# Two transformer layers and a mixture block in float32: the norms in front of the feed-forward parts are applied after the product instead of before it

## The reference, cut to what matters

```
def rms_norm(x, g):
    y = x * rsqrt(mean(x * x, axis=-1) + EPS)
    return y * g
def modulate(h, shift, scale):
    return h * (1 + scale) + shift
def swiglu(h, w_in, w_out):
    a, u = split(h @ w_in, 2)
    return (silu(a) * u) @ w_out

x  = x + g1 * (merged @ w_o)
h2 = modulate(rms_norm(x, norm2), sh2, sc2)
x  = x + g2 * swiglu(h2, w_ffn_in, w_ffn_out)
```

## Time and profile before

| | |
|---|---|
| median of 3 runs | 3013.39 us (3013.12 to 3019.73) |
| profiled execution, its own time | 3018.23 us |
| its span (first to last instruction) | 3016.3 us |
| TensorE busy | 2892.8 us, 96% of the span |
| mean granted TensorE clock | 0.985 of full |

### The profile page before, as it was taken

The page is one execution under the profiler, slowest core; times in us unless marked ns, Lnnn a source line. Parts: engine busy times, 40 slices in busy tenths (PEclk is TensorE's granted clock), DMA queues, the critical chain, the costliest instruction groups (busy, mean ns, idle before and its releaser), DMA issues.

```text
span 3016.3 us, 40764 instructions
## 1 busy us (share of the span) xinstructions
PE 2892.8 (96%) x16464; PEld 2148.1 (71%) x16464; DVE 954.1 (32%) x1413; ACT 959.0 (32%) x1668; POOL 800.2 (27%) x624
## 2 busy tenths in 40 slices
PE   8999889999999999999988999999999999999998
PEld 6887668888888888878766777888854644444444
DVE  3505551122211111051453123212367532322324
ACT  3226442123221122242544223222355331212114
POOL 2323222324222322443222444444420300000000
PEclk8999999999999999999999999999999999999999
DMA  5114321111111211212322222232220369999990
GB/s 211 56 67 168 111 90 57 63 63 56 59 64 58 66 68 48 70 56 81 133 96 71 84 85 92 87 106 98 91 90 28 146 257 409 408 401 408 401 374 28
DMA packets 60681, 407.55 MB, mean 135 GB/s; under 512 B 7008, under 2 KB 7408, under 8 KB 16528
## 3 DMA queue, kind: packets, MB, share of 16 engines
q1 hardware_dynamic: 58400, 397.96, 35.3%
q0 software_dynamic: 1872, 6.72, 0.6%
q10 hardware_dynamic: 288, 1.16, 0.1%
HBM read 403.71 MB, written 2.10 MB: 135 GB/s over the span
## 4 chain that ended last, share of the span: by engine, by line
PE 82%; issue 8%; POOL 3%; DVE 3%; ACT 3%; DMA 1%; SPq 0%; POOLq 0%; DVEq 0%; ACTq 0%
PE ps L636 46%; PE ps L1189 7%; PE ps L1212 4%; PE ps L880 3%; POOL half_slots L1802 3%; PE ps L907 3%; PE ps L861 3%; PE ps L1231 2%; PE ps L1261 2%; PE ps L667 2%; PE ps L1155 2%; PE ps L646 2%; PE ps L694 1%; PE ps L1044 1%; DMA mod_head_low<-stream 1%
## 5 line engine op out<-in xcount | busy, mean ns | idle before, releaser
L636 PE MATMUL ps<-h_parts,half_slots 128*128 128x512 f32 (+1 forms) x5520 | 1067.6, 355 | 15.0 <-POOL half_slots L1802 14.6
L636 PEld LDWEIGHTS ps<-h_parts,half_slots 128*128 128x128 f32 x5520 | 906.7, 189 | 173.5 <-issue 13.7
L1802 POOL TENSOR_TENSOR half_slots<-ring,half_slots 128x1024 fp32r<-128x1024 f32 (+3 forms) x276 | 590.2, 2139 | 1102.3 <-ACT half_slots L1328 1101.9
L1328 ACT ACTIVATE half_slots<-ring 128x1024 fp32r<-128x1024 f32 (+3 forms) x276 | 263.4, 955 | 1251.2 <-PE ps L636 1239.2
L636 PE MATMUL ps<-hidden_parts,half_slots 128*128 128x512 f32 (+1 forms) x1584 | 305.1, 355 | 0.0
L636 PEld LDWEIGHTS ps<-hidden_parts,half_slots 128*128 128x128 f32 x1584 | 261.0, 188 | 43.6
L636 PE MATMUL ps<-y_parts,half_slots 128*128 128x512 f32 (+1 forms) x1152 | 229.2, 359 | 9.9 <-DVE y_parts L2140 9.7
L1189 PE MATMUL ps<-second_block,scratch 128*64 128x512 f32 x1024 | 223.3, 594 | 1.9 <-ACT scratch L1719 1.4
L636 PEld LDWEIGHTS ps<-y_parts,half_slots 128*128 128x128 f32 x1152 | 192.8, 191 | 44.3 <-issue 11.7
L1189 PEld LDWEIGHTS ps<-second_block,scratch 128*64 128x64 f32 x1024 | 74.5, 137 | 143.4 <-issue 143.4
L2193 DVE TENSOR_TENSOR first_block<-ps,first_block 128x768 f32<-128x768 f32 (+1 forms) x44 | 36.3, 825 | 428.7 <-PE ps L636 413.8
(11 more groups left out here) (340 smaller groups left out, 3056.9 us busy)
## 6 DMA issues: line engine op xcount, KB each, us to landing
second_block<-experts SPq DMA_DIRECT2D x192, 1024.0 KB, 9.0
ring<-stream SPq DMA_DIRECT2D x138, 1024.0 KB, 4.8
ring<-stream SPq DMA_DIRECT2D x16, 768.0 KB, 4.2
ring<-stream SPq DMA_DIRECT2D x16, 640.0 KB, 3.9
ring<-stream SPq DMA_DIRECT2D x16, 512.0 KB, 3.6
mod_head_low<-stream SPq DMA_DIRECT2D x6, 1024.0 KB, 19.6
first_block<-bias POOLq DMA_DIRECT2D x16, 384.0 KB, 4.5
second_block<-w_gate SPq DMA_DIRECT2D x4, 1024.0 KB, 7.9
```

The lines of the kernel that those rows point to most:

```text
L636: last = nc.tensor.matmul(ps[s % 2][:, a:b], part(x, s)[:, k, :], parts[y][:, tile + k, a:b], start=start and k == 0 and n == 0, stop=stop ...
L1328: act.activation(part(0, s), raw_half(s), ACT.Copy).then_inc(hi_done, 1)
L1802: nc.gpsimd.tensor_tensor(part(1, s), raw_half(s), part(0, s).bitcast(fp32), ALU.subtract)\
```

## The change

The operand of the feed-forward input is no longer the normed tile but x times its column scale, `norm2 * (1 + sc2)`, in upper and lower part (`HF`). It is made tile by tile while `w_o` still runs (`gain_upper_x` on ACT, `gain_lower_x` on DVE). The shift goes in as two further columns of the operand (tokens and context), so that the product of weights and shift comes out in two columns of PSUM. [...] The sums over features and the spreading of 1/rms are put between tiles of the first two half products. The spread 1/rms is copied to `RF`. DVE evicts both halves of each pair times `RF` and takes the shift columns out; ACT applies SiLU with the shift as bias; DVE adds the other shift and multiplies in one instruction. The interleaved first pair, the third weight slot and the busywork around these two norms go. Semaphores that other parts count too (`y2_hi`, `m_act`, `m_g`, `rs_kept`) get offsets there.

```diff
@@ -259,6 +261,10 @@
         NG = SQ
+        HF = [view(x_parts, i * KD * (T + 2), KD, T + 2) for i in range(2)]
+        RF, UF, AF = SQ[:, 0, :], SQ[:, 1, :], CG
+        SHIFT = T
+        shifts = small[:, 0, :]
         TM = view(B, 4608, 4, T)
@@ -440,6 +446,24 @@
+        def shifted_pieces(nt):
+            first = 512 if nt == T else 256
+            return [(0, first, 0), (first, nt + 2, 512)]
+        def grouped(ap, nt):
+            return ap if nt == T else ap.rearrange("p (b n) -> p b n", n=256)
+        def in_bank(bank, nt):
+            whole = bank[:, 0:1024].rearrange("p (b n) -> p b n", n=512)
+            return bank[:, 0:nt] if nt == T else whole[:, :, 0:256]
+        def tile_kinds(nt):
+            return [(0, 0, NL), (1, NL, nt)][:2 if nt == T else 1]
         NGS = {n: NG if n < 4 else (NG3, NG2, NG2)[n - 4] for n in range(7)}
@@ -631,9 +654,9 @@
                         ready(k)
-                    for a, b in pieces(nt):
+                    for a, b, to in spans or [(a, b, a) for a, b in pieces(nt)]:
                         for n, (x, y) in enumerate(((0, 0), (0, 1), (1, 0))):
-                            last = nc.tensor.matmul(ps[s % 2][:, a:b], part(x, s)[:, k, :], parts[y][:, tile + k, a:b],
+                            last = nc.tensor.matmul(ps[s % 2][:, to:to + b - a], part(x, s)[:, k, :], parts[y][:, tile + k, a:b],
                                                     start=start and k == 0 and n == 0,
@@ -722,11 +745,15 @@
                     stay_busy(2)
+                spread_rstd(n, nt)
+            def spread_rstd(n, nt):
                 pe.wait_ge(rstd_ok, 2 * n + 2)
...
                 last.then_inc(spread, 1)
-                if n in (1, 2, 3):
+                if n == 2:
                     stay_busy(5)
@@ -964,18 +991,27 @@
-                spread_sum(2 * l + 1, nt)
+                def first_half(k):
+                    pe.wait_ge(y2_lo, (KD + 1) * l + k + 2)
+                    if k == 2:
+                        sum_seven(2 * l + 1, nt)
+                    elif k == 4:
+                        sum_last(2 * l + 1, nt)
+                def second_half(k):
+                    if k == 3:
+                        spread_rstd(2 * l + 1, nt)
                 for hf in range(2):
...
                         for j in range(2 * j0, 2 * j1):
-                            if hf == 0 and j == 0:
-                                first_pair(s0, nt, h_tile(2 * l + 1))
-                            if hf == 0 and j < 2:
-                                continue
                             half_free(s0 + j, 4, i)
-                            product(s0 + j, HS, nt, 4, i)
+                            product(s0 + j, HF, nt, 4, i, spans=shifted_pieces(nt),
+                                    ready=(first_half, second_half)[j] if hf == 0 and j < 2 else None)
@@ -1508,11 +1544,20 @@
+                def gain_upper_x(m):
+                    for kind, a, b in tile_kinds(nt):
+                        last = act.activation(HF[0][:, m, a:b], X[:, m, a:b], ACT.Copy, scale=amod[:, 2 * l + 1, m, kind:kind + 1])
+                    last.then_inc(y2_hi, 1)
                 for m in range(KD):
...
                     squares(2 * l + 1, nt, [m])
+                    if m == 0:
+                        act.wait_ge(mod_ready, 2 * l + 2)
+                        act.activation(HF[0][:, :, nt:nt + 2], mod[:, 48 * l + 24:48 * l + 32, :], ACT.Copy).then_inc(y2_hi, 1)
+                    gain_upper_x(m)
                 root(2 * l + 1, nt)
-                upper_h(l, 1, nt)
@@ -1522,17 +1567,21 @@
                             upper(s + 2, 4, i)
-                            act.wait_ge(steps, 4 * i + (s + 1))
-                            if j >= 2:
-                                act.wait_ge(gs_lo, 2 * i + (done + j - 1))
-                            act.activation(RAW[:, j % 2, 0:nt], ps[0][:, 0:nt], ACT.Silu).then_inc(evac["A"], 1)
+                            if hf == 0 and j == 0:
+                                act.wait_ge(spread, 2 * l + 2)
+                                act.activation(RF[:, 0:nt], ps[2][:, 0:nt], ACT.Copy).then_inc(rs_kept, 1)
+                            act.wait_ge(evac["V"], ev("V", s, 4, i))
+                            for kind, a, b in tile_kinds(nt):
+                                c = 4 * (j % 2) + kind
+                                last = act.activation(AF[:, j % 2, a:b], AF[:, j % 2, a:b], ACT.Silu, bias=shifts[:, c:c + 1])
+                            last.then_inc(m_act, 1)
                             upper(s + 3, 4, i)
-                            act.wait_ge(evac["V"], ev("V", s + 1, 4, i))
+                            act.wait_ge(m_g, 2 * i + (done + j + 1))
                             if isinstance(i, int):
-                                dst, src = GS[0][:, j, 0:nt], RAW[:, j % 2, 0:nt]
+                                dst, src = GS[0][:, j, 0:nt], AF[:, j % 2, 0:nt]
                             else:
-                                dst, src = GS[0][:, ds(2 * i + j, 1), 0:nt], RAW[:, j % 2:j % 2 + 1, 0:nt]
+                                dst, src = GS[0][:, ds(2 * i + j, 1), 0:nt], AF[:, j % 2:j % 2 + 1, 0:nt]
                             act.activation(dst, src, ACT.Copy).then_inc(gs_hi, 1)
@@ -1886,7 +1935,6 @@
                     lower(2 * SLOT0[l, "w_o"] + m + 2)
-                lower_h(2 * l + 1, ntq)
                 for hf in range(2):
@@ -2175,9 +2223,24 @@
+                def gain_lower_x(m):
+                    dve.wait_ge(y2_hi, (KD + 1) * l + m + 2)
+                    for kind, a, b in tile_kinds(nt):
+                        last = nc.vector.scalar_tensor_tensor(out=HF[1][:, m, a:b], in0=X[:, m, a:b],
+                                                              scalar=amod[:, 2 * l + 1, m, kind:kind + 1],
+                                                              in1=HF[0][:, m, a:b].bitcast(fp32), op0=ALU.mult, op1=ALU.subtract)
+                    last.then_inc(y2_lo, 1)
                 for m in range(8):
                     update(2 * SLOT0[l, "w_o"] + m, 16, m)
-                times_rstd(2 * l + 1, nt)
+                    if m == 0:
+                        dve.wait_ge(y2_hi, (KD + 1) * l + 1)
+                        nc.vector.tensor_tensor(HF[1][:, :, nt:nt + 2], mod[:, 48 * l + 24:48 * l + 32, :],
+                                                HF[0][:, :, nt:nt + 2].bitcast(fp32), ALU.subtract).then_inc(y2_lo, 1)
+                    gain_lower_x(m)
+                rstd(2 * l + 1, nt)
+                dve.wait_ge(rs_kept, l + 1)
@@ -2186,17 +2249,30 @@
                         for j in range(j0, j1):
-                            s = s0 + 2 * j + 1
+                            s = s0 + 2 * j
+                            b = j % 2
+                            rows, scale = AF[:, b, 0:nt], grouped(RF[:, 0:nt], nt)
                             dve.wait_ge(steps, 4 * i + (s + 1))
-                            dve.wait_ge(evac["A"], ev("A", s, 4, i))
-                            g = RAW[:, j % 2, 0:nt]
-                            nc.vector.tensor_tensor(g, ps[1][:, 0:nt], g, ALU.mult).then_inc(evac["V"], 1)
+                            if done + j > 1:
+                                dve.wait_ge(gs_lo, 2 * i + (done + j - 1))
+                            nc.vector.tensor_copy(shifts[:, 4 * b:4 * b + 2], ps[0][:, SHIFT:SHIFT + 2])
+                            nc.vector.tensor_tensor(grouped(rows, nt), in_bank(ps[0], nt), scale, ALU.mult).then_inc(evac["V"], 1)
+                            dve.wait_ge(steps, 4 * i + (s + 2))
+                            nc.vector.tensor_copy(shifts[:, 4 * b + 2:4 * b + 4], ps[1][:, SHIFT:SHIFT + 2])
+                            nc.vector.tensor_tensor(grouped(UF[:, 0:nt], nt), in_bank(ps[1], nt), scale, ALU.mult).then_inc(evac["V"], 1)
+                            dve.wait_ge(evac["V"], ev("V", s + 1, 4, i))
+                            dve.wait_ge(m_act, 2 * i + (done + j + 1))
+                            for kind, a, z in tile_kinds(nt):
+                                c = 4 * b + 2 + kind
+                                last = nc.vector.scalar_tensor_tensor(out=AF[:, b, a:z], in0=UF[:, a:z], scalar=shifts[:, c:c + 1],
+                                                                      in1=AF[:, b, a:z], op0=ALU.add, op1=ALU.mult)
+                            last.then_inc(m_g, 1)
                             dve.wait_ge(gs_hi, 2 * i + (done + j + 1))
                             if isinstance(i, int):
-                                dst, hi = GS[1][:, j, 0:nt], GS[0][:, j, 0:nt]
+                                dst, hi, g = GS[1][:, j, 0:nt], GS[0][:, j, 0:nt], AF[:, b, 0:nt]
                             else:
                                 dst, hi = GS[1][:, ds(2 * i + j, 1), 0:nt], GS[0][:, ds(2 * i + j, 1), 0:nt]
-                                g = RAW[:, j % 2:j % 2 + 1, 0:nt]
+                                g = AF[:, b:b + 1, 0:nt]
```

(37 more changed lines are left out.)

4 lines of the change are left out of this document (2 added, 2 removed).

## The result

Over 13 runs each, side by side, the changed kernel takes 3023.76 us (median, 3017.4 to 3026.89) and the kernel before 3017.31 us. The ratio is 1.0018, 95% interval 1.001 to 1.0025, some 5.4 us slower (the interval is 3.0 to 7.5 us). A second comparison (11 and 14 runs, the last experiment) gave 1.0009, 1.0 to 1.0018, some 2.7 us. The forecast was -0.8 us, 3012.6 us, with a range up to 3022. The change in time lies within 0.3%, as the likeliest case said, but on the other side of nothing, and the time lies outside the range. Of that, 3.9 us are the kernel before itself, whose median was 3013.39 in the three runs shown.

What follows compares the result with a forecast made beforehand. TensorE, busy for 96% of the span, was taken to bound the kernel. Stall -16.4, split +12.0, shift columns +0.9 and +0.9, w_o +1.8 gave -0.8 us on 3013.39: 3012.6 us, range 3001 to 3022.

Steps and rivals of the forecast that it cites:

- the likeliest case: Whole kernel: -0.8 us to 3012.6 us, own range 3007 to 3018, chance 0.55; within 0.3% of before, chance 0.61.
- The stall: Norms before the feed-forward inputs: TensorE's stops go, saving 9.7 us in layer 0 and 6.75 in layer 1, 16.4 together.
- waits (a) to (c): Layer 1's norm: last x tile, root with 1/rms, and first PSUM eviction all come early enough; smallest cover about 2 us.
- The split: Layer 1's feed-forward inputs: 512 columns become 256 + 258, 0.238 us a pair, +12.0 us, two extra columns 0.9 more.
- the run of three: Matmul starts 800.35, 800.46, 800.58, then 800.70 in the old trace: 0.11, 0.12, 0.12 us; source for 0.119 a matmul.
- The faster rival: Layer 1's split: 256 columns cost half of 512, 0.113 us, so the split is free; 3000.6 us, chance 0.2.
- The slow rival: Layer 1's split: weight loads bind 256 columns at 0.123 us or more; 3022 us at 0.1233, 3027 at 0.126; chance 0.14.
- The two columns in layer 0: Layer 0's feed-forward inputs: second matmul grows from 256 to 258 columns, 0.9 ns on 1056 matmuls, +0.9 us.
- w_o in layer 1: DVE's new subtraction comes during POOL's sum and delays POOL's weight part at every second product, +1.8 us.
- The longer eviction: Feed-forward inputs: additional DVE and ACT work per pair of half products stays hidden, 1.6 us to spare in layer 1; costs nothing.
- The sum: All terms: -16.4 + 12.0 + 0.9 + 0.9 + 1.8 = -0.8 us, from the median 3013.39 to 3012.6 us.

Runs made afterwards that it cites:

- the last experiment: The changed kernel run again unaltered, for the spread; ratio 1.0009 (1.0 to 1.0018) to the kernel before.
- experiment 3: Kernel before with 42 half products of layer 1's feed-forward inputs cut into 256 + 256 columns; ratio 1.0041, +12.4 us, second input 127.32 us.
- experiment 1: Changed kernel without the two shift columns, rows still 770; second feed-forward input 185.42 us in layer 0, 123.07 in layer 1.
- 9: Changed kernel without shift columns, rows of 768; second feed-forward input 184.80 us in layer 0, 120.33 in layer 1.
- experiment 2: Changed kernel with operand rows of 784 instead of 770 columns; second feed-forward input 185.97 us in layer 0, 127.33 in layer 1.
- 5: Changed kernel without shift columns, rows of 784; second feed-forward input 185.09 us in layer 0, 122.93 in layer 1.
- Experiment 4: Changed kernel with DVE's subtraction in w_o issued one tile later, when POOL stands idle; layer 1's w_o 52.12 us instead of 53.40.
- experiments 10: Kernel before with two more DVE instructions per pair of half products in layer 1; its second feed-forward input 120.33 us, as before.
- 11: Changed kernel without shift columns, rows of 784, evictions of the kernel before; second feed-forward input 185.09 us in layer 0, 122.93 in layer 1.

## Why the prediction was off, step by step

- **The stall:** right in mechanism and size. The excess of the first input over the second went from 13.60 to 3.99 us in layer 0 (9.6 saved, 9.7 forecast) and from 8.70 to 2.03 in layer 1 (6.7 saved, 6.75 forecast). None of the waits (a) to (c) bound. What the prediction did not see is that 3.4 us of the old stall in layer 0 run at a granted clock of 0.50. It counted them with the rest, rightly, as they went with it; how much of the 9.6 us is the clock was not separated.
- **The split:** 2 x 6.13 = 12.3 us for 1056 pairs against 12.9 forecast with its two columns, 0.119 us a matmul as taken from the run of three. That this came out so close is in part luck. The split alone costs 13.2 ns a pair (experiment 3), 14.0 us for 1056 pairs, where 12.0 were forecast; rows of 770 gave 0.9 us back at each input, which nobody had foreseen. The faster rival (0.113) is refuted by 120.0 ns in a stream of nothing else. The slow rival's 0.1233 stood on 512-column matmuls that keep their 226.7 ns in layer 0; they take 232.1 there, and the 256 beside them 117.9. My reason for the 0.119, a bound by weight loads, is not needed: the same 13 ns above 2.4 columns a ns stand at 512 columns and some 14 to 16 at 384 and 386. At 256 columns it isn't excluded, for there the records of the weight loader leave no gap (115.00 of the 115.00 us from 2015 in the changed kernel, 95.22 before).
- **The two columns in layer 0: the step that failed.** "By columns that is 2/512 of 0.2267, 0.9 ns" came to 0.9 us; measured are 2 x 2.35 = 4.7 us. Two things are in it. The first is the distance between rows, which the columns bring and which the step left out: 0.62 us an input for 770 instead of 768, without the columns (experiment 1 against 9). The second is the columns themselves: 1.73 us an input on top of that (the changed kernel against experiment 1), and 0.88 with rows of 784 (experiment 2 against 5), where their width gives 0.47. So pricing by width was too low even at the better distance. I had no row for either: every operand of such a product in the kernel before has rows of 768 and 256 or 512 columns. Why the chip is slower there stays open.
- **w_o in layer 1:** 1.5 us (1.4 in the second profile) against 1.8. Experiment 4 takes 1.3 of it away and so shows that much to come from DVE's subtraction falling into POOL's sum (1.26 us for 0.74, and POOL's weight part 2.83 for 2.39); 0.25 us stay.
- **The longer eviction:** nothing, as forecast. The output halves are unchanged; experiments 10 and 11 show that half as much DVE work again, or the old evictions, leave the stream as it is.
- **The sum:** the terms measured give +2.2 us in place of -0.8; the difference is the failed step (3.8) and 0.2 at the stall, less 0.6 at the split and 0.3 at w_o. By layer it is -4.9 us in layer 0 and +7.1 in layer 1. The timed runs say 5.4 and 2.7 us; 2.2 is inside the interval of the second comparison and below that of the first (3.0 to 7.5). What lies between 2.2 and 5.4 isn't settled. The stretches at a granted clock of 0.50 fall differently (96.2 us of them in the profile after, 89.3 before, 102.9 in the second), and with them stages differ also between two profiles of the same kernel: from the first to the second of the changed one layer 0's w_o grows by 1.4 us with 3.4 us more of them, and what follows layer 1 by 3.1 us with 6.7 more. No experiment ties them to the change.
- **The time itself:** 3.9 us of the 11.2 by which the median missed are the median of three runs that I started from.

## What to carry to other kernels

Deferring a norm behind the product paid what its stall cost (9.6 and 6.7 us here), and that was read to 0.1 us from the excess of the first product over a later one. What it adds to the operand had to be priced per matmul and not by width. Here each further matmul cost 13.2 ns on unchanged rows, which ate the gain where 512 columns became 514. Two further columns cost two to four times their width, and a new distance between rows cost up to 5 ns a matmul in one stream and 0.5 to 1.2 ns a pair in the other. So take such a change where its columns fit into the matmuls that are there, and leave it out where it splits them: layer 0 alone with even cuts is 0.2% faster than before, both layers are 0.1 to 0.2% slower. Whether the shift columns cost less when the rows stay 768 apart, with the columns kept elsewhere, was not tried.

## What was not expected of the hardware

- In a stream of nothing but 512-column float32r matmuls one takes 226.7 ns with operand rows 768 columns (3072 bytes) apart and 231.7 on average with 784 (231.9 with 770), all else the same. It does not carry over to other streams. Where 512 and 256 columns alternate, rows of 768 already give 232.1 + 117.9 ns a pair, and 784 adds 0.5 ns. Where matmuls are of 256 columns, 768 and 784 are equal (127.32 us for 1056 of 256, 127.33 with 258 in every second) and 770 is the better one (126.46). So it isn't simply a matter of a start at a multiple of 64 bytes. The cause is not known, and no other distance was tried.
- With rows of 768, in streams of one width, 256 columns take 120.0 ns and 512 take 226.7: by the estimate of experiment 3, 13.3 ns a matmul beside 2.4 columns a ns. 384 and 386 columns, alternating on rows of 784, lie 1.2 and 2.4 ns above that line.
- With the old norm TensorE's granted clock falls to 0.50 for 3.4 us in layer 0's norm (in one of the three profiles for two such stretches); with the new one, in none of the eleven profiles.
